# Layer 1's cached values: one unsplit float32 product for four sequences at a time, in place of split products for one sequence

## The reference, cut to what matters

```python
idx = n_past + jnp.arange(t_len)[:, None] - dil * steps[None, :]
kg = k_cat[:, idx]
vg = v_cat[:, idx]
scores = jnp.einsum('btkgd,btjkd->btkgj', q, kg) * dh ** -0.5
...
p, lse = softmax_lse(scores, sink)
o = jnp.einsum('btkgj,btjkd->btkgd', p.astype(v_cat.dtype), vg)
...
wts = jax.nn.softmax(jnp.stack(lses), axis=0)
o = jnp.sum(wts[..., None] * jnp.stack(outs).astype(jnp.float32), axis=0)
```

## Time and profile before

| | us |
|---|---|
| median of 3 runs | 2610.78 (2606.39 to 2613.58) |
| the profiled execution, its own time | 2608.77 |
| its span, first to last instruction | 2607.0 |
| TensorE busy with matmuls | 2342.5 (90%) |
| VectorE busy | 1545.8 (59%) |
| ScalarE busy | 812.4 (31%) |
| GpSimd busy | 422.9 (16%) |

### The profile page before, as it was taken

One profiled execution on the slowest core, in us unless ns is written; L12 is line 12 of the kernel. 1 busy time (PEld: TensorE's weight loads), 2 busy tenths in 40 slices (PEclk: granted clock), 3 DMA queues, 4 the chain that ended last, 5 costly groups with the idle time before them and its releaser, 6 DMA issues.

```text
span 2607.0 us, 41605 instructions
## 1 busy us (share of the span) xinstructions
PE 2342.5 (90%) x17224; PEld 2171.6 (83%) x17224; DVE 1545.8 (59%) x2261; ACT 812.4 (31%) x1608; POOL 422.9 (16%) x289
## 2 busy tenths in 40 slices
PE   7998987779899999999979888978988886999997
PEld 7897776668789999999978778877877755999997
DVE  5885776775645543445645775677576656543444
ACT  4333322354343212213123332423333343221221
POOL 1000222211110100000342242143134301000000
PEclk9999989879899999999999989989999868999998
DMA  4226666553235878777585675467367632877874
GB/s 152 81 75 208 225 242 243 196 163 109 74 121 176 277 250 273 258 257 243 185 268 171 195 247 186 152 207 263 106 196 253 213 112 97 289 245 257 276 256 180
DMA packets 284320, 519.94 MB, mean 199 GB/s; under 512 B 19184, under 2 KB 255072, under 8 KB 280288
## 3 DMA queue, kind: packets, MB, share of 16 engines
q1 hardware_dynamic: 272816, 324.45, 38.9%
q10 hardware_dynamic: 5888, 177.91, 18.7%
q0 software_dynamic: 5440, 15.08, 1.7%
HBM read 483.76 MB, written 210.80 MB: 266 GB/s over the span
## 4 chain that ended last, share of the span: by engine, by line
PE 58%; DVE 18%; DMA 7%; issue 7%; ACT 7%; POOL 2%; SPq 1%; DVEq 0%; ACTq 0%; POOLq 0%
PE gp L2292 31%; PE gp L2820 7%; DMA uk<-in_dil_k 5%; PE gp L2616 5%; PE gp L2440 3%; POOL uq L2920 2%; DVE cacc L1579 2%; DVE vs L2175 2%; DVE sc_t L2101 2%; DMA decay<-tmp_a_row 2%; ACT w_hi L1336 1%; DVE w_lo L2012 1%; PE mp L2707 1%; PE mp L2782 1%; PE mp L2676 1%
## 5 line engine op out<-in xcount | busy, mean ns | idle before, releaser
L2292 PE MATMUL gp<-a_hi,w_hi 128*128 128x272 f32 x1456 | 306.1, 291 | 25.8 <-DVE w_lo L1502 12.8
L2292 PE MATMUL gp<-a_lo,w_hi 128*128 128x272 f32 x1456 | 302.5, 289 | 0.0
L2292 PE MATMUL gp<-a_hi,w_lo 128*128 128x272 f32 x1456 | 301.5, 289 | 0.0
L2920 POOL TENSOR_TENSOR uq<-uq,uk 128x1024 f32<-128x1024 f32 x96 | 240.9, 2511 | 318.7 <-DMA uk<-in_dil_k 318.3
L2820 PE MATMUL gp<-a_hi,w_hi 128*128 128x272 f32 x1152 | 260.2, 308 | 1.4 <-DVE v_st L2034 1.4
L2292 PEld LDWEIGHTS gp<-a_hi,w_hi 128*128 128x128 f32 x1456 | 231.0, 189 | 28.6 <-DVE w_lo L1502 12.8
L2820 PE MATMUL gp<-a_hi,w_lo 128*128 128x272 f32 x1152 | 246.0, 296 | 0.0
L2820 PE MATMUL gp<-a_lo,w_hi 128*128 128x272 f32 x1152 | 245.2, 295 | 0.0
L2292 PEld LDWEIGHTS gp<-a_hi,w_lo 128*128 128x128 f32 x1456 | 230.3, 190 | 0.0
L2292 PEld LDWEIGHTS gp<-a_lo,w_hi 128*128 128x128 f32 x1456 | 228.5, 190 | 0.0
L2820 PEld LDWEIGHTS gp<-a_hi,w_hi 128*128 128x128 f32 x1152 | 195.9, 198 | 23.8 <-issue 3.7
(11 more groups left out here) (382 smaller groups left out, 4592.9 us busy)
## 6 DMA issues: line engine op xcount, KB each, us to landing
out_dil_ks<-in_dil_k ACTq DMA_DIRECT2D x32, 2044.0 KB
out_dil_vs<-in_dil_v ACTq DMA_DIRECT2D x32, 2044.0 KB
uq<-tmp_rows SPq DMA_DIRECT2D x96, 512.0 KB, 4.4
w_raw<-in_odd_w_in SPq DMA_DIRECT2D x36, 1024.0 KB, 7.9
w_raw<-in_w_up SPq DMA_DIRECT2D x32, 1024.0 KB, 7.8
w_raw<-in_w_down SPq DMA_DIRECT2D x32, 1024.0 KB, 8.1
uk<-in_dil_k SPq DMA_DIRECT2D x64, 512.0 KB, 6.1
v_raw<-in_dil_v SPq DMA_DIRECT2D x128, 256.0 KB, 3.3
```

Source lines behind the costliest of these rows:

```text
L2292: m = nc.tensor.matmul(gp[:, c, h, 0:HALF], w[:, sl, k, c * P:(c + 1) * P], x[:, k, h * HALF:(h + 1) * HALF], start=n < 2, stop=n >= 46)
L2920: nc.gpsimd.tensor_tensor(uq[:, n % 2], uq[:, n % 2], k, ALU.mult).then_inc(item_mul, 1)
```

## The change

The cached values are no longer split. A unit is now one tile (group and token offset) for four sequences: one load of 512 KB (128 partitions, 4 sequences, 256 columns of float32) straight into `vs`, and four matmuls, one for each sequence j, which write partitions 32j to 32j+31 of the same bank. There are 9 units for each half of the sequences, 18 in a quarter in place of 40. The halves of the sequences take the two halves of the bank's 512 columns. The probabilities stay float32 as well: the step `st` writes them straight from PSUM into `p_all` and `p_pad` for all eight sequences, and `pad`, `sp_t` and both `split_v` are gone. `sum_v` becomes a copy of 128x256, twice in a quarter instead of eight times. The ring is 3 buffers of 512 KB for quarters 0 to 2. For quarter 3 it is 15: the 11 places of before, and the four item buffers once the last items are done.

```diff
-UNITS = [(0, 0), (1, 0), (1, 2), (2, 0), (2, 2)]
-N_UNITS = len(UNITS) * NB
-N_RING = (3, 3, 3, 11)
+TILES = [(0, 0)] + [(g, t) for g in (1, 2) for t in range(NT)]
+N_HALF = len(TILES)
+N_UNITS = 2 * N_HALF
+N_RING = (3, 3, 3, 15)
+def unit(U):
+    return U // N_UNITS, U % N_UNITS // N_HALF, *TILES[U % N_HALF]
...
-        per, offsets = ((12, (0, 2, 5, 7, 9)), (14, (0, 2, 5, 8, 10)), (14, (0, 2, 5, 8, 10)), (7, (0, 1, 2, 3, 4)))[qd]
-        places = [(b + 22 + (n + 1) // 8, (n + 1) % 8) for n in (per * u + off for u in range(NB) for off in offsets)]
+        per = (5, 6, 6, 2)[qd]
+        places = [(b + 22 + (n + 1) // 8, (n + 1) % 8) for n in (per * u + 6 * (u >= N_HALF) for u in range(N_UNITS))]
...
     load_v(U), SyncE:
-                if U % 40 >= N_RING[qd]:
+                if U % N_UNITS >= N_RING[qd]:
                     sp.wait_ge(v_mm, U - N_RING[qd] + 1)
                 elif RING[U] < 3:
-                    wait(sp, v_mm, 40 * qd)
+                    wait(sp, v_mm, N_UNITS * qd)
+                elif RING[U] < 11:
+                    sp.wait_ge(mm_done, chunk0(ENTRY["o", 0, 2]))
+                elif RING[U] < 13:
+                    sp.wait_ge(item_mul, 96)
                 else:
-                    sp.wait_ge(mm_done, chunk0(ENTRY["o", 0, 2]))
+                    sp.wait_ge(item_done, 96)
-                n = 2 if g else 1
-                src = a[f"dil{g}_v"][b].rearrange("(i r) f -> i r f", r=DIL[g])[:, t:t + n, cols]
-                sp.dma_start(v_raw[RING[U]][:, 0:n, 1], src).then_inc(v_in[RING[U]], 16)
+                src = a[f"dil{g}_v"][4 * half:4 * half + 4].rearrange("b (i r) f -> r i b f", r=DIL[g])[t, :, :, cols]
+                sp.dma_start(vs[RING[U]][:, :], src).then_inc(v_in[RING[U]], 16)
...
     small_out("st"), ScalarE:
-                    nc.scalar.activation(sp_t[:].rearrange("p a b -> p (a b)"), M[:, 0:384], ACT.Copy)
+                    wait(act, v_mm, N_UNITS * qd)
+                    nc.scalar.activation(p_all[:, :, 0:16].rearrange("p b (h t) -> p b h t", h=4),
+                                         M[:, 0:P].rearrange("p (h b t) -> p b h t", h=4, b=NB), ACT.Copy)
+                    for g in (1, 2):
+                        nc.scalar.activation(pad_rows(g), M[:, g * P:(g + 1) * P].rearrange("p (h n) -> p h n", h=4), ACT.Copy)
...
     sum_v(U), VectorE:
-                nc.vector.tensor_reduce(sv_t[32 * (b % 4):32 * (b % 4) + 32],
-                                        mp[0:32, 2].rearrange("p (l f) -> p f l", l=2), AX.X, ALU.add).then_inc(sv_sum, 1)
+                nc.vector.tensor_copy(sv_t, mp[:, 2, 256 * half:256 * half + 256]).then_inc(sv_sum, 1)
...
     times_unit(U), TensorE:
-                if U % 5 == 0:
-                    wait(pe, sv_sum, 8 * qd + b)
-                    pe.wait_ge(pad_done, K + 1)
-                pe.wait_ge(v_lo, U + 1)
-                for i in range(2 if g else 1):
-                    at = 4 + 32 * (8 * (b % 2) + 4 * (g - 1) + t0 + i) - (t0 + i)
-                    lhs = p_pad[K % 2][:, at:at + 32] if g else p_all[:, K % 2, b % 2]
-                    m = nc.tensor.matmul(mp[0:32, 2], lhs, vs[RING[U]][:, i].rearrange("p l f -> p (l f)"), start=U % 5 == 0,
-                                         stop=(U % 5, i) == (4, 1), skip_group_check=True)
+                if U % N_HALF == 0:
+                    wait(pe, sv_sum, 2 * qd + half)
+                    pe.wait_ge(small_done, NTH["st", qd, 0] + 1)
+                pe.wait_ge(v_in[RING[U]], 16 * USES[U])
+                for j in range(4):
+                    b = 4 * half + j
+                    at = 4 + 16 * (NS * (g - 1) + NT * b + t) - t
+                    lhs = p_pad[:, at:at + 32] if g else p_all[:, b]
+                    m = nc.tensor.matmul(mp[32 * j:32 * j + 32, 2, 256 * half:256 * half + 256], lhs, vs[RING[U]][:, j],
+                                         start=(g, t) == TILES[0], stop=(g, t) == TILES[-1], skip_group_check=True)
                 m.then_inc(v_mm, 1)
```

More of the change, by code:

```diff
@@ L303, in when @@
     return "early" if part <= 2 else "mid" if part < 6 else "late"
-SPLIT_AT, SUM_AT = {}, {}
+SUM_AT = {}
 for _u, (_s, _p) in UNIT_AT.items():
-    SPLIT_AT.setdefault((_s - 1, "late") if _p <= 2 else (_s, "early") if _p < 6 else (_s, "mid"), []).append(_u)
-    if _u % 5 == 4:
+    if _u % N_HALF == N_HALF - 1:
         SUM_AT.setdefault((_s, when(_p)), []).append(_u)
@@ L502, in build @@
         uk = over_a("uk", [P, 2, NT, 2 * P])
[L503 to L507 removed]
+        vs.append(over_a("vs1", [P, 4, 2 * P]))
+        p_pad = over_a("p_pad", [P, 4 + 2 * NB * NT * 16 + 28])
+        p_all = over_a("p_all", [P, NB, 32])
         vn1 = over_a("vn1", [3 * NS, 2 * P])
@@ L640, in build @@
         smx_done = sem("smx_done")
-        v_in = [sem(f"v_in{n}") for n in range(11)]
-        v_hi = sem("v_hi")
-        v_lo = sem("v_lo")
+        v_in = [sem(f"v_in{n}") for n in range(N_RING[3])]
         v_mm = sem("v_mm")
-        pad_hi = sem("pad_hi")
-        pad_done = sem("pad_done")
         sv_sum = sem("sv_sum")
@@ L1456, in _ @@
                     small_out(kind, qd, x)
-                for U in SPLIT_AT.get((z, "late"), ()):
-                    split_v(U)
             split_odd(len(ODD) - 1)
@@ L1992, in tables @@
             def tables():
-                for t in p_pad:
-                    nc.vector.memset(t[:].bitcast(F32), 0.0)
-                pairs = ident[:].rearrange("p (j h l t) -> p h j l t", j=4, h=4, l=2)
-                nc.vector.tensor_tensor(pick[:].rearrange("p h (j t) -> p h j t", j=4), pairs[:, :, :, 0], pairs[:, :, :, 1], ALU.add)
+                nc.vector.memset(p_pad[:], 0.0)
+                nc.vector.memset(p_all[:], 0.0)
+                nc.vector.tensor_copy(pick[:].rearrange("p h (j t) -> p h j t", j=4),
+                                      ident[:].rearrange("p (j o h t) -> p o h j t", j=4, o=2, h=4)[:, 0])
                 dve.wait_ge(c1_in, 16 * 17)
@@ L2235, in _ @@
                     factors_out(SLOT0.index(z - 27))
-                for K in PAD_AT.get(z, ()):
-                    pad(K)
-                for U in SPLIT_AT.get((z, "late"), ()):
-                    split_v(U)
                 for U in SUM_AT.get((z, "late"), ()):
```

82 lines of the change are left out of this document (14 added, 68 removed).

## The result

The changed kernel takes **2513.79 us** (median, 2512.78 to 2514.76) beside 2612.18 us of the kernel before; the ratio is 0.9625 with an interval of 0.9606 to 0.9644. A second set gave 2518.04 us and 0.9631 [0.9618, 0.9644].

The account below looks back on a forecast made before the run. TensorE, busy for 90% of the span, was taken as the bound, so time could come from its work or idle time. 2608.8 - 6 - 30 - 22 = 2551 us, median 2553 us; range 2522 to 2600.

Parts of the forecast that it names:

- TensorE's own work: Value-product units: 0.79 us each with four quarters overlapping, 2.1 us less a quarter, -6 us over three quarters.
- rival by the strict order: Matmuls start strictly in program order, so a unit takes 1.43 us and the kernel 2599 us; chance 0.04.
- The three stretches: Value products of quarters 0 to 2 beside the next quarter's items: fewer TensorE waits for VectorE, -30 us, bounds -15 and -60.
- crowded entries: Entries making the prompt's softmax factors, VectorE busy nearly throughout: its removed work comes back whole, about 7 us a quarter, 22 together.
- the remaining 38 us: TensorE's other waits in the stretches, where items press: a quarter counted as won, 9 us.
- the bound of -60: Far bound of the stretches' term: all 60 us of TensorE's waits for VectorE's splits and sums are won.
- The items take over: Rival for the stretches: waits for splits become waits for items, -30 becomes about 0, 2583 us; chance 0.08.
- ScalarE "counts nothing by itself": In the stretches ScalarE's removed work gains nothing, since it is busy 59.19 of 166 us and the rest hides there.
- The tail: After the stretches: score periods -10 us, last score to merge -14 us; -22 us taken, bounds -10 and -30.
- New waits: Value loads wait until the unit three before is used; twice as large with twice the time, priced at nothing.
- Two-fold overlap: Rival: only two partition quarters overlap, a unit costs 1.21 us; stretches 22 and tail 8 us more, 2583 us; chance 0.18.
- No overlap: Rival: quarters do not overlap, a unit costs 2.07 us; slower, 2630 to 2645 us; chance 0.08.

Follow-up runs that it names:

- e5_chain_fill: e3_chain with 152 matmuls of TensorE's own, results thrown away, in 21 of its waits in front of units; 2599.2 us.
- e9_light_keys: The changed kernel loading one row of four of the cached keys in two items of three, sample scores partly left out; 2497.2 us.
- e14_chain_act: e3_chain without VectorE's maxima: only ScalarE's two copies stand ahead of each unit, and TensorE waits for them; 2543.8 us.
- e8_small_loads: The changed kernel with each 512 KB load of values as four loads of 128 KB; 2521.7 us.
- e17_late_again: The changed kernel with value loads one slot later in SyncE's queue, except in the last quarter; a repeat run, 2507.7 us.
- e1_serial: The changed kernel with all four products of a unit on partitions 0 to 31, that part of the result left wrong; 2574.5 us.
- e3_chain: The changed kernel with two ScalarE copies, then two VectorE maxima, put back ahead of each unit, and TensorE waiting for these; 2597.7 us.
- e6_fill_tail: The changed kernel with seven float32 128x512 matmuls, results thrown away, in the last merge's wait of 7 us; 2523.3 us.

## Why the prediction was right in direction and too small

**TensorE's own work, -6.** Right. The unit measured 0.77 us, so three quarters give 3 x (16.3 - 18 x 0.77) = 7 us. The Trainium skill, "TensorE: Matmul & The Clock Gate", Part 3, gives a speedup of 2.38 for three column tiles, from which the prediction estimated about 3.2 for four; these runs have 1.85 / 0.57 = 3.2. The rival by the strict order that the same part states made a unit 1.43 us, and is not borne out by 0.77.

**The three stretches, -30.** This is the step that failed. It was read from TensorE's idle time: 22 us for the crowded entries, and "of the remaining 38 us I count a quarter". The idle time did fall by 29.5 us, in part by luck: in the three entries with the factors it fell by 15 us and not by 22, elsewhere by 14.5 and not by 9. And the stretches, beyond the units' 7 us, fell by 50. The other 21 us stood in the trace as busy time of TensorE; by the ratio of the clocks, an estimate, 447 us at a granted clock near 0.92 are some 18 us longer than at 0.96. e5_chain_fill shows that this isn't a second price which the clock charges, but the same wait seen from the other side: the passes set the length, and TensorE fills it by being idle or by being slow. The right base for the term was not the 60 us of waits but all by which the stretch exceeded its work at full clock, or, from the passes' side, what they hold up in their queues. With the bound of -60 the working had the value in hand; it took a point nearer the other end and left "a stretch term near -60" out of the range.

**The items take over.** Partly right: the wait for `e` grew, and e9_light_keys nearly removes it. Its price is small, 17 us in all for three quarters of the bytes of two items in three, and the same with and without the passes.

**ScalarE "counts nothing by itself".** Wrong. At 29% busy it costs 30 us to give its passes back (e14_chain_act): 12 us in the stretches, for which the sentence was written, and 16 in the tail.

**The tail, -22.** Right in direction, too small by 8 us, and at the far bound of -30. The periods are 5.2 us against 6.8, the last piece 15.7 us against 18. In the periods a unit has no large matmul beside it and takes 0.57 us to the next instruction's start, not 0.79; four of them are 0.9 us of the 1.6. The rest is mostly less waiting, of which 0.3 to 0.8 us a period are left. That TensorE would run mostly at full clock in the periods was right, and it weighs much: 20.6 of the 29.6 us are TensorE's busy time, and the units' own work at full clock makes up only 6 of these (16.3 - 18 x 0.57). For the last piece the working priced VectorE's path to the factors; put back alone, VectorE's passes cost the tail 4 us and ScalarE's 16.

**New waits, nothing.** No unit waited for its load, so this held; what the load's size is worth stays within a few us of nothing (e8_small_loads). The queue behind the loads was not free: held back less, it gives 10 us (e17_late_again). The change had not brought this wait: from 1600 to 2000 us SyncE stood 192.1 us at value buffers before, and 153.7 after.

**The rivals.** Two-fold overlap: its unit (1.19 us measured, 1.21 worked out) was right where it was made, but its price of 30 us came out as 13. No overlap was to be the other side, 2630 to 2645 us, with the sign turning at 1.6 us a unit; at 2.04 us a unit e1_serial took 2574 us. The sign didn't hang on the overlap, since the passes were worth more than the forecast gave them.

**Open.** The two pieces between the stretches lost 6.7 us, for which the forecast had nothing. They are back at 122.0 us in e3_chain (122.2 before), at 119.8 with ScalarE's passes alone and at 115.5 with VectorE's alone; the changed kernel has 115.5 and 116.8. So this too goes with the passes, ScalarE's above all; by which wait is not shown. About 14 us of the 98 are in none of the passes put back; the units' 2.4 us a quarter are 10 of them, and e3_chain puts back less work than the change took. That e6_fill_tail was 7.6 us slower in code that it shares with the changed kernel shows how far two builds can be apart.

## What to carry to other kernels

Where a wait is read from an engine's idle time, read its granted clock in the same windows. In the stretches, where other engines set the pace, the time that a slower clock filled was part of the wait and went with it; in the tail, in whose periods TensorE is busy for 84 to 90%, the clock set much of the length. To price passes on helper engines, put them back one engine at a time; here they added up (51 and 30 us) although the engines were only 55% and 29% busy. An in-order DMA queue that waits at a buffer still in use delays all loads behind it: one slot's shift of an issue was worth 10 us.

## What was not expected of the hardware

Float32 products of 128x256 in one, two and four partition quarters took 1.85, 0.99 and 0.57 us for eight records: the overlap is nearly in proportion. Among large matmuls a unit costs 0.20 us more than that in each of the three (0.77, 1.19 and 2.04 us). After 7 us without work, eight records of 128x128 took 1.80 to 2.07 us instead of 1.05, in all four such groups at 0.58 granted; that was 3.4 us in all.
